# Expert gathers of a PEER layer on one core: down and up rows issued in alternating groups of four instead of eight

## The chip, the cores and the metric

One Trainium2 chip, one of its cores. The metric is the device time of one execution in microseconds (us); less is better.

## What is computed

One decoder layer for a prompt of 512 tokens and eight sample tokens: two parallel token mixers, then a PEER channel mixer, then a final norm. The change touches only PEER. For each token and each of eight heads a product-key search finds 16 experts out of 16,384. Each expert is one row of 1,024 fp32 numbers (4 KB) in `expert_down` and one in `expert_up`:

```python
    def block(xb):
        qv = (xb @ w_query).astype(f32).reshape(PEER_BLOCK, PEER_HEADS, 2, PEER_DHALF)
        s = jnp.einsum('thsd,hskd->thsk', qv, keys)
        sv, si = lax.top_k(s, PEER_TOPK)
        ...
        g = jax.nn.softmax(fv, axis=-1)
        u = expert_down[eidx]
        act = jax.nn.gelu(jnp.einsum('thkd,td->thk', u, xb).astype(f32), approximate=False) * g
        v = expert_up[eidx]
        return jnp.einsum('thk,thkd->td', act.astype(v.dtype), v)
```

## The kernel before

The program runs six stages, one after another. The last one, `stage_peer` (line 1527), begins some 975 us into the span and lasts to its end.

Its work is cut into 33 units. A unit is one head of one block of 128 tokens (4 blocks x 8 heads = 32), and between unit 19 and the one after it stands one unit for the samples, whose 8 tokens x 8 heads x 16 experts are 1,024 rows. A unit of the prompt has two steps of eight experts each, the samples' unit has one step, so there are NSTEP = 65 steps, numbered n = 0 to 64; the samples' step is n = 40. Step n needs eight down gathers D(n) and eight up gathers U(n). One gather is one indirect DMA issued by POOL: 128 rows of 4 KB, one into each partition, 512 KB. There are 520 of each kind.

What sets the order:

- **POOL** issues all gathers. In a loop over n it issues the eight of D(n) (`gather_down`, L1674), then the eight of U(n-4) (`gather_up`, L1694); LAG is 4. In the last step it issues D(64), then U(60) to U(64). Before the first gather of a unit it waits until the unit's expert numbers stand (`s_top`). Before every second down gather it waits until the buffer is free; down rows have a ring of 10 buffers in the first block and of 12 after it. Before the up gathers 0 and 4 of a step it waits until the same half of the eight up buffers has been used (`s_vused`).
- **DVE** multiplies each gathered down row with the token's row and sums (`products`, L1924, one instruction for one gather). For every unit it also picks the next unit's experts: `topk`, some 45 small instructions, of which L1916 writes the expert numbers. Its order in a unit is: products of the first step, stores of scores (L1371, first block only), `close` of a token block if one is due (L1944, L1946), topk of the next unit, products of the second step.
- **ACT** applies gelu and exp and spreads the weights into a diagonal form.
- **PE** multiplies the up rows with these weights and adds them up in PSUM (`add`, L1809; L1817 for the samples), four gathers to a half, with `s_vused` raised after each half. add(n-4) runs in step n. In the first block PE also projects and scores the queries of coming units (L1344, L1358): in an even step n up to 12 it scores two tiles through one PSUM bank before add(n-4), and the second score waits for DVE's store of the first. In step 14 it scores the samples and waits for DVE's copies after products(14) (L1987), then selects the samples' rows (L1826, L1828), then runs add(10).
- A token block is closed by DVE in steps 20, 36 and 53, after the products of that step: the multiply L1944 reads the PSUM banks that the next block's first add (add(16), add(32), add(49)) overwrites, and PE waits for it (`s_blkrd`).
- **SP** loads the query weights for the next units (1 MB each) and stores the closed blocks.

Of the kernel before, what the change touches and what calls it, by code (L numbers as in the profile page):

```python
# [55 lines left out]
PH = 8  # L56
# [1465 lines left out]
GATE = 8  # L1522
LAG = 4
VR = 8


def stage_peer(nc, mem, sem, ps, A, O, mod_d, integers):
# [54 lines left out]
    S = 2 * NU  # L1582
# [20 lines left out]
    at_step = {n: [n - LAG] for n in range(LAG, NSTEP)}  # L1603
# [3 lines left out]
    V_before = [max([m for m in range(n) if V_of[m] == V_of[n]], default=None) for n in range(NSTEP)]  # L1607
# [18 lines left out]
    with nc.Block() as block:  # L1626
        @block.sync
        def _(sp):
            for i in range(2, PH):
                if i > 2:  # L1630
                    sp.wait_ge(s_q, 2 * (i - 2))
                Q.load(sp, A, i).then_inc(s_w[i % 2], 16)
            sp.wait_ge(s_s, NQ)
            for dst, m in ((gate, 5), (shift, 6), (scale, 7)):
                sp.dma_start(dst[:, 0, :], mod_d[NS:NC_ROWS, m * D:(m + 1) * D].partition_broadcast(P)).then_inc(s_rows, 16)
                sp.dma_start(dst[0:NS, 1, :], mod_d[0:NS, m * D:(m + 1) * D]).then_inc(s_rows, 16)
            sp.dma_start(gf, A["g_final"].rearrange("(a n) -> a n", a=1).partition_broadcast(P)).then_inc(s_rows, 16)

            for i, b in enumerate(closings):
                sp.wait_ge(s_y, i + 1)  # L1640
                if b < NB:
                    sp.dma_start(O[0][0, b * P:(b + 1) * P, :], yb).then_inc(s_out, 16)
                else:
                    sp.dma_start(O[1].rearrange("b s d -> (b s) d"), yb[0:NS, :]).then_inc(s_out, 16)
            sp.wait_ge(s_out, 16 * (NB + 1))

        @block.gpsimd
        def _(pool):
            G = nc.gpsimd
            link = Link(pool, s_pc)  # L1650
            link(G.memset(Z, 0.0))
            link(G.memset(sel, 0.0))
            link(G.affine_select(out=sel, in_=sel, compare_op=ALU.not_equal, fill=1.0, base=0,
                                 pattern=[[0, 2 * PH], [-1, NS]], channel_multiplier=1))
            G.iota(iotai, pattern=[[1, TOPK]], base=0, channel_multiplier=0).then_inc(s_const, 1)  # L1655

            def gather_down(n):

                g = steps[n]
                u = unit_at[g]  # L1660
                if g == S or g % 2 == 0:
                    pool.wait_ge(s_top, u + 1)
                    pool.sem_inc(s_gatep, 1)
                if n == 2 * PH:
                    pool.wait_ge(s_ss, 1)
                    pool.sem_inc(s_gatep, 1)
                for j in range(GATE):
                    i = GATE * n + j
                    if j % 2 == 0 and U_free[i + 1] is not None:
                        pool.wait_ge(s_uused, U_free[i + 1] + 1)  # L1670
                        pool.sem_inc(s_gatep, 1)
                    k = (g % 2) * GATE + j
                    at = idxS[:, j:j + 1] if g == S else idx[u % 2][:, k:k + 1]
                    G.indirect_dma_start(U[i], None, down, bass.IndirectOffsetOnAxis(ap=at, axis=0))\  # L1674
                        .then_inc(s_U[U_sem[i][0]], 16)

            def gather_up(n):

                g, r = steps[n], V_of[n]
                if g != S and g % 4 == 0:  # L1680
                    pool.wait_ge(s_idxT, g // 4 + 1)
                    pool.sem_inc(s_gatep, 1)
                if r and V_before[n] is None:
                    pool.wait_ge(s_uused, GATE * NSTEP)
                    pool.sem_inc(s_gatep, 1)
                for j in range(VR):
                    if j % 4 == 0 and V_before[n] is not None:
                        pool.wait_ge(s_vused, 2 * V_before[n] + 1 + j // 4)
                        pool.sem_inc(s_gatep, 1)
                    if g == S:  # L1690
                        at = idxS[:, j:j + 1]
                    else:
                        at = idxT[(g // 4) % 2][:, VR * (g % 4) + j:VR * (g % 4) + j + 1]
                    G.indirect_dma_start(Vr[r][j], None, up, bass.IndirectOffsetOnAxis(ap=at, axis=0))\  # L1694
                        .then_inc(s_V[r][j], 16)

            for n in range(NSTEP):
                gather_down(n)
                for m in at_step.get(n, ()):
                    gather_up(m)  # L1700

        @block.scalar
        def _(act):
# [371 lines left out]
```

## Time and profile before

| | us |
|---|---|
| median of 3 runs | 2418.75 |
| lowest and highest | 2417.25, 2419.3 |
| the profiled execution | 2418.92 |
| its span, from its first to its last instruction | 2417.2 |
| PE, DVE, POOL busy in it | 1329.5, 1501.2, 1071.5 |
| DMA issued by POOL (queue q0) | 545.33 MB |

The span is cut by the page into 40 slices of 60.4 us; the mean busy share of the core's 16 DMA engines stands at 9 tenths or more in nearly every slice from the 19th on, which is where the gathers run. Matmul times are modelled by the profiler, and a DMA's landing is seen as the start of the instruction that waits for it.

### The profile page before, as it was taken

To read this page: it belongs to the slowest core of one execution; us is meant where nothing else is said; L and a number is where in the kernel's file an instruction comes from. 1 tells how busy PE (TensorE), PEld (TensorE's weight loads), DVE (VectorE), ACT (ScalarE), POOL (GpSimd) and SP (SyncE) were. 2 spreads that over 40 slices of the span, in tenths; PEclk is the share of its full clock that TensorE was granted. 3 is DMA by queue.
4 is the path that set the end of the run, shared out by engine and by line. 5 is a ranking of instruction groups with operands and counts; after the bars stand their busy time and mean duration, and the time that the engine had idled before them with its cause. 6 is when DMAs were issued, how large, how long until landed. Compare 5 with 4: busy or idle time off the path is not lost.

```text
span 2417.2 us, 19658 instructions
## 1 busy us (share of the span) xinstructions
PE 1329.5 (55%) x6380; PEld 763.6 (32%) x6380; DVE 1501.2 (62%) x3220; ACT 278.7 (12%) x567; POOL 1071.5 (44%) x1138
## 2 busy tenths in 40 slices
PE   3597997999754789656654333323332343232234
PEld 0276764778644654543431000000000010000000
DVE  0453999145488423686676777767686677676740
ACT  1111000111211002111110110000011011010100
POOL 0123000010031000357666777777775777777754
PEclk7898998899766999878885555566565565656657
DMA  9821100211133050589999999999998999999997
GB/s 365 320 64 67 39 35 0 90 40 72 53 96 129 12 193 1 183 334 405 406 403 409 409 402 409 410 409 405 406 406 319 409 384 409 409 410 409 409 369 287
DMA packets 208777, 651.97 MB, mean 270 GB/s; under 512 B 25936, under 2 KB 52208, under 8 KB 204537
## 3 DMA queue, kind: packets, MB, share of 16 engines
q0 software_dynamic: 149760, 545.33, 57.1%
q1 hardware_dynamic: 58092, 103.70, 12.0%
q10 hardware_dynamic: 824, 1.70, 0.2%
q8 instruction: 51, 0.84, 0.1%
q14 instruction: 50, 0.41, 0.0%
HBM read 643.24 MB, written 7.54 MB: 269 GB/s over the span
## 4 chain that ended last, share of the span: by engine, by line
DMA 20%; POOL 17%; issue 10%; DVE 8%; PE 4%; DVEq 1%; ACT 0%; POOLq 0%; ACTq 0%
DMA arena<-in_expert_up_dram,rows 13%; POOL arena L1694 9%; POOL arena L1674 8%; DMA arena<-in_expert_down_dram,expert 6%; DVE arena L1924 4%; PE ps L1809 3%; DMA arena<-in_expert_down_dram,sample 1%; DVE arena L1878 0%; DVE arena L1877 0%; DVEq L1871 0%; PE ps L1344 0%; PE ps L1358 0%; DVE keys L1876 0%; DVE arena L1905 0%; DVE arena L1902 0%
## 5 line engine op out<-in xcount | busy, mean ns | idle before, releaser
L1809 PE MATMUL ps<-arena 128*32 128x512 f32 x2048 | 413.4, 950 | 792.0 <-DMA arena<-in_expert_up_dram,rows 792.0
L1924 DVE CUSTOM_DVE_ANT_0 arena<-arena,ps 128x1024 f32<-128x1024 f32 x512 | 617.0, 1220 | 319.7 <-DMA arena<-in_expert_down_dram,expert 304.3
L1694 POOL DMA_INDIRECT arena<-in_expert_up_dram,rows x512 | 486.6, 950 | 217.0 <-issue 136.4
L1674 POOL DMA_INDIRECT arena<-in_expert_down_dram,expert x512 | 487.3, 952 | 207.2 <-issue 151.0
L1809 PEld LDWEIGHTS ps<-arena 128*32 128x32 f32 x2048 | 82.3, 147 | 1084.6 <-issue 1084.4
L546 PE MATMUL ps<-arena 128*128 128x260 f32 x896 | 204.9, 388 | 14.4 <-ACT arena L477 7.8
L546 PEld LDWEIGHTS ps<-arena 128*128 128x128 f32 x896 | 171.6, 193 | 51.1 <-issue 16.2
L954 POOL MEMSET arena<- 128x528 f32 x2 | 1.1, 537 | 305.5 <-POOLq L2044 305.5
L1344 PE MATMUL ps<-arena 128*128 128x260 f32 x512 | 123.9, 403 | 5.0 <-POOL counting L1655 3.6
L1071 PE MATMUL ps<-arena 128*128 128x260 f32 x512 | 112.5, 383 | 0.0
L1344 PEld LDWEIGHTS ps<-arena 128*128 128x128 f32 x512 | 101.8, 202 | 27.8 <-issue 5.1
L1071 PEld LDWEIGHTS ps<-arena 128*128 128x128 f32 x512 | 97.3, 190 | 14.8
L1714 ACT ACTIVATE arena<-arena 128x8 f32<-128x8 f32 x65 | 13.5, 208 | 729.4 <-DVE arena L1924 729.3
L970 POOL TENSOR_TENSOR arena<-arena 128x1024 f32<-128x1024 f32 x8 | 18.2, 2286 | 166.7 <-DVE arena L1230 127.1
L1460 PE MATMUL ps<-arena 128*128 128x512 f32 (+1 forms) x160 | 71.6, 611 | 7.9 <-DMA arena<-in_w_out_dram 7.9
L269 PE MATMUL ps<-arena 128*32 128x512 f32 x256 | 45.9, 855 | 47.2 <-DMA arena<-in_w_ada_dram 38.3
L1167 PE MATMUL ps<-arena 128*128 128x260 f32 x256 | 57.4, 388 | 0.0
L456 POOL MEMSET arena<- 128x4096 f32 x1 | 3.5, 3512 | 113.0 <-POOLq L2044 113.0
L469 POOL COPY arena<-arena 64x16 f32<-64x16 f32 x64 | 31.7, 547 | 48.2 <-DVE arena L720 48.1
L1167 PEld LDWEIGHTS ps<-arena 128*128 128x128 f32 x256 | 49.6, 194 | 7.8
L607 PE MATMUL ps<-arena 128*128 128x512 f32 x64 | 39.4, 751 | 21.1 <-DVE arena L737 12.6
L1419 POOL MEMSET arena<- 128x1024 f32 x1 | 1.0, 956 | 111.2 <-POOLq L2044 111.2
(352 smaller groups left out, 1858.1 us busy)
## 6 DMA issues: line engine op xcount, KB each, us to landing
arena<-in_w_ada_dram SPq DMA_DIRECT2D x12, 2048.0 KB, 19.7
arena<-in_w_in_dram SPq DMA_DIRECT2D x11, 2048.0 KB, 7.6
arena<-in_w_ada_final_dram SPq DMA_DIRECT2D x4, 2048.0 KB, 17.8
arena<-in_w_query_dram SPq DMA_DIRECT2D x8, 1024.0 KB, 16.9
arena<-in_expert_down_dram,expert POOLq DMA_INDIRECT x512, 12.3
arena<-in_expert_up_dram,rows POOLq DMA_INDIRECT x512, 12.0
out_dram<-arena SPq DMA_DIRECT2D x13, 512.0 KB, 3.0
arena<-in_x_prompt_dram SPq DMA_DIRECT2D x2, 2048.0 KB
```

What stands on the lines that cost most here:

```text
L269: last = nc.tensor.matmul(ps[strip(j, 32), i, :], cT[:, k, :], ring[q][:, k % 2, 512 * j:512 * j + 512], start=(k == 0), stop=(k == KD - 1))
L469: last = nc.gpsimd.tensor_copy(flat[:, 160 * q + 16 * g:160 * q + 16 * g + 16], bb[rows, j, 4 * ut + q, :])
L546: last = nc.tensor.matmul(ps[:, 5 + h, 0:HALF], ring[i % 2][:, k, m * P:(m + 1) * P], hT[:, k, h * HALF:(h + 1) * HALF], start=(k == 0), s ...
L607: last = nc.tensor.matmul(ps[:, 7, :], CT[j][:, i, :], S_of(i)[j].rearrange("p a b -> p (a b)"), start=(q == 0 and j == 0), stop=(q == 3 a ...
L1071: last = mm(ps[:, 2 * (n % 2) + h, 0:HALF], ring[i % 2][:, k, m * P:(m + 1) * P], hT[:, k, h * HALF:(h + 1) * HALF], start=(k == 0), stop= ...
L1167: last = mm(ps[:, 4 + 2 * (m % 2) + h, 0:HALF], brw[:, k, m * P:(m + 1) * P], cv[:, k, h * HALF:(h + 1) * HALF], start=(k == 0), stop=(k = ...
L1344: last = nc.tensor.matmul(ps[:, 2 + h, 0:HALF], self.ring[(t // 2) % 2][:, k, (t % 2) * P:(t % 2 + 1) * P], self.h2T[:, k, h * HALF:(h + 1 ...
L1460: last = mm(ps[0:n, 2 * (b % 2) + j, :], mg[:, k, b * P:b * P + n], wo[:, k, j * 512:(j + 1) * 512], start=(k == 0), stop=(k == KD - 1))
L1674: G.indirect_dma_start(U[i], None, down, bass.IndirectOffsetOnAxis(ap=at, axis=0))\
L1694: G.indirect_dma_start(Vr[r][j], None, up, bass.IndirectOffsetOnAxis(ap=at, axis=0))\
L1809: last = mm(ps[32 * j:32 * j + 32, c, :], Z[:, j, m, :], Vr[r][4 * half + j][:, c * 512:(c + 1) * 512], start=(p % 4 == 0 and m == 0), sto ...
L1924: V.tensor_tensor_reduce(U[i], U[i], row, 1.0, 0.0, ALU.mult, ALU.add, dots[n % 2][:, j:j + 1]).then_inc(s_uused, 1)
```

## The change

`gather_down` and `gather_up` take a part, 0 or 1, and issue four gathers instead of eight. In steps 4 to 63 POOL now issues D(n) 0-3, U(n-4) 0-3, D(n) 4-7, U(n-4) 4-7. In steps 0 to 3 there are no up gathers, and in step 64 D(64) is issued whole and then U(60) to U(64), each whole, so the order in those five steps is as before. The waits that stand ahead of a step's gathers go with part 0; the waits for buffers stay with their gathers. No buffer, semaphore, count or other engine's program is changed.

```diff
-            def gather_down(n):
+            def gather_down(n, part):
...
-                if g == S or g % 2 == 0:
+                if part == 0 and (g == S or g % 2 == 0):
                     pool.wait_ge(s_top, u + 1)
...
-                for j in range(GATE):
+                for j in range(4 * part, 4 * part + 4):
...
-            def gather_up(n):
+            def gather_up(n, part):
...
-                for j in range(VR):
+                for j in range(4 * part, 4 * part + 4):
                     if j % 4 == 0 and V_before[n] is not None:
                         pool.wait_ge(s_vused, 2 * V_before[n] + 1 + j // 4)
...
             for n in range(NSTEP):
-                gather_down(n)
-                for m in at_step.get(n, ()):
-                    gather_up(m)
+                up_now = at_step.get(n, ())
+                for part in range(2):
+                    gather_down(n, part)
+                    if len(up_now) == 1:
+                        gather_up(up_now[0], part)
+                if len(up_now) > 1:
+                    for m in up_now:
+                        for part in range(2):
+                            gather_up(m, part)
```

## Rows read from the trace of the kernel before

**Rows 1.** The page: the span, and what POOL's DMA queue carried (packets, MB, share).

```profile
span 2417.2 us, 19658 instructions
...
q0 software_dynamic: 149760, 545.33, 57.1%
```

**Rows 2.** Busy time by window: PE, PEld, DVE, ACT, POOL, PE clock, DMA share, GB/s.

```profile
1500.00:1510.00 10.00, 1.00 (x8) 0.40 (x12) 9.18 (x30) 1.49 (x2) 7.56 (x9) 0.52 1.03 409
...
1840.00:1850.00 10.00, 6.03 (x28) 1.37 (x32) 8.01 (x33) 1.29 (x7) 0.06 (x1) 0.50 0.16 66
1850.00:1860.00 10.00, 1.25 (x8) 0.00 (x0) 4.30 (x7) 2.29 (x7) 7.56 (x9) 0.50 0.81 278
...
1950.00:1960.00 10.00, 2.79 (x16) 0.54 (x16) 8.86 (x33) 4.37 (x9) 7.87 (x8) 0.72 0.82 277
```

**Rows 3.** POOL's waits for PE from 980 us: total us, times, longest us.

```profile
POOL arena L1694 <- PE ps L1809: 63.7, 50, 10.7
```

**Rows 4.** Timeline, an ordinary even step: start us, us, engine, line [idle before <- releaser].

```profile
1515.20 0.17 DVE L1916 CAST expert<-arena 128x16 uint32<-128x16 f32 x1
...
1522.30 0.94 POOL L1694 DMA_INDIRECT arena<-in_expert_up_dram,rows  x1 [0.30 <-issue]
1523.55 0.94 POOL L1674 DMA_INDIRECT arena<-in_expert_down_dram,expert  x1 [0.31 <-issue]
...
1535.75 1.22 DVE L1924 CUSTOM_DVE_ANT_0 arena<-arena,ps 128x1024 f32<-128x1024 f32 x1 [10.28 <-DMA arena<-in_expert_down_dram,expert]
```

**Rows 5.** Timeline, the samples' unit: last product, next experts, next down gather, its products.

```profile
1837.49 1.23 DVE L1924 CUSTOM_DVE_ANT_0 arena<-arena 128x1024 f32<-128x1024 f32 x1
...
1848.87 0.17 DVE L1916 CAST expert<-arena 128x16 uint32<-128x16 f32 x1
...
1849.94 0.93 POOL L1674 DMA_INDIRECT arena<-in_expert_down_dram,expert  x1 [12.91 <-DVE expert L1916]
...
1854.30 1.22 DVE L1924 CUSTOM_DVE_ANT_0 arena<-arena,ps 128x1024 f32<-128x1024 f32 x1 [5.02 <-DMA arena<-in_expert_down_dram,expert]
...
1864.66 1.22 DVE L1924 CUSTOM_DVE_ANT_0 arena<-arena,ps 128x1024 f32<-128x1024 f32 x1
```

**Rows 6.** Timeline, the samples' up rows on PE and POOL's next up gathers.

```profile
1933.31 15.45 PE L1817 MATMUL ps<-arena 128*8 128x512 f32 x31 [12.85 <-DMA arena<-in_expert_up_dram,sample]
...
1943.13 0.94 POOL L1694 DMA_INDIRECT arena<-in_expert_up_dram,rows  x1 [3.35 <-PE ps L1817]
...
1948.60 0.59 PE L1817 MATMUL ps<-arena 128*8 128x512 f32 x1
...
1950.00 0.94 POOL L1694 DMA_INDIRECT arena<-in_expert_up_dram,rows  x1 [2.20 <-PE ps L1817]
```

**Rows 7.** Timeline, step 14: last product, add(10), and add(11) one step later.

```profile
1294.35 1.22 DVE L1924 CUSTOM_DVE_ANT_0 arena<-arena,ps 128x1024 f32<-128x1024 f32 x1
...
1299.92 3.64 PE L1809 MATMUL ps<-arena 128*32 128x512 f32 x16
...
1320.98 3.64 PE L1809 MATMUL ps<-arena 128*32 128x512 f32 x16 [12.67 <-DMA arena<-in_expert_up_dram,rows]
```

**Rows 8.** Timeline, step 20: the closing multiply, add(16), and add(17) one step later.

```profile
1420.14 1.22 DVE L1944 TENSOR_TENSOR arena<-ps,arena 128x1024 f32<-128x1024 f32 x1
...
1424.24 3.64 PE L1809 MATMUL ps<-arena 128*32 128x512 f32 x16 [11.93 <-DMA arena<-in_expert_up_dram,rows]
...
1445.51 3.64 PE L1809 MATMUL ps<-arena 128*32 128x512 f32 x16 [12.89 <-DMA arena<-in_expert_up_dram,rows]
```

**Rows 9.** Timeline, step 10: last product, second score, add(6), and add(7).

```profile
1205.28 1.22 DVE L1924 CUSTOM_DVE_ANT_0 arena<-arena,ps 128x1024 f32<-128x1024 f32 x1
...
1207.33 2.05 PE L1358 MATMUL ps<-arena 128*128 128x128 f32 x8 [2.84 <-DVE arena L1371]
1210.51 3.49 PE L1809 MATMUL ps<-arena 128*32 128x512 f32 x16 [1.13 <-DMA arena<-in_expert_up_dram,rows]
...
1230.97 3.50 PE L1809 MATMUL ps<-arena 128*32 128x512 f32 x16 [6.21 <-DMA arena<-in_expert_up_dram,rows]
```

More of the change, by code:

```diff
@@ L1655, in _ @@
             G.iota(iotai, pattern=[[1, TOPK]], base=0, channel_multiplier=0).then_inc(s_const, 1)
-            def gather_down(n):
+            def gather_down(n, part):
                 g = steps[n]
                 u = unit_at[g]
-                if g == S or g % 2 == 0:
+                if part == 0 and (g == S or g % 2 == 0):
                     pool.wait_ge(s_top, u + 1)
                     pool.sem_inc(s_gatep, 1)
-                if n == 2 * PH:
+                if part == 0 and n == 2 * PH:
                     pool.wait_ge(s_ss, 1)
                     pool.sem_inc(s_gatep, 1)
-                for j in range(GATE):
+                for j in range(4 * part, 4 * part + 4):
                     i = GATE * n + j
@@ L1675, in gather_down @@
                         .then_inc(s_U[U_sem[i][0]], 16)
-            def gather_up(n):
+            def gather_up(n, part):
                 g, r = steps[n], V_of[n]
-                if g != S and g % 4 == 0:
+                if part == 0 and g != S and g % 4 == 0:
                     pool.wait_ge(s_idxT, g // 4 + 1)
                     pool.sem_inc(s_gatep, 1)
-                if r and V_before[n] is None:
+                if part == 0 and r and V_before[n] is None:
                     pool.wait_ge(s_uused, GATE * NSTEP)
                     pool.sem_inc(s_gatep, 1)
-                for j in range(VR):
+                for j in range(4 * part, 4 * part + 4):
                     if j % 4 == 0 and V_before[n] is not None:
```

## The prediction

> **What bounds the kernel now.** I read the page first, then busy time by window, then POOL's waits, then the timeline at the places where those two views disagree with an even flow. The page gives POOL's queue 545.33 MB [rows 1]; nothing in the change alters that. In an ordinary window the 16 DMA engines stand at a share of 1.03 and move 409 GB/s [rows 2]. At that rate one gather of 524,288 bytes takes 1.28 us. POOL starts one every 1.25 us [rows 4], a little faster, so it runs ahead until it meets a buffer that isn't free. Its waits for PE, 63.7 us in 50 of them [rows 3], are mostly this: a symptom of full DMA engines, not a cause of lost time. So the stage is bound by bytes through the DMA engines, and a wait of POOL costs time only if the engines run out of issued gathers.
>
> They do so in a few places. Around the samples, in 1840 to 1860, they moved 66 and 278 GB/s where 409 was possible: (818 - 344) / 409 x 10 = 11.6 us lost [rows 2]. In 1950 to 1960 they moved 277: (409 - 277) / 409 x 10 = 3.2 us lost [rows 2]. Another loss lies in the last step and one at the start of the stage, in whose steps the order isn't changed. I therefore look for the change's effect in two forms only: gathers that are late at a place where the engines already run dry, and places that newly run dry.
>
> **What the change moves.** It removes and adds no instruction. Gathers go through the engines in the order of issue, so I count in places of 1.28 us. Within a step the down gathers 4-7 are now four places later (+5.1 us) and the up gathers 0-3 four places earlier (-5.1 us); the others stay. From this follow two kinds of effect: what waits for the last down row of a step comes 5.1 us later, and POOL asks for the first half of the up buffers 5.1 us earlier. The distance from one use of an up buffer to the next stays 16 places, and from one use of a down buffer to the next it becomes more even, so where a buffer's user starts at landing nothing changes.
>
> **Ordinary steps: nothing.** The next unit's experts are written at 1515.20, and POOL wants them at 1523.55, 8.2 us later [rows 4]. The chain that writes them starts with the last down row, so the slack falls to about 3 us in ordinary units. Where it is less (steps with a close, or PE's scores in between) POOL may wait 1 to 3 us. But a gather's product starts 1535.75 - 1523.55 = 12.2 us after its issue [rows 4]: some eight issued gathers stand in line ahead of it, and the engines don't notice such a wait. I cost it at 0; without that cover each such wait would cost its 1 to 3 us.
>
> **The samples' unit: +5.1 us.** This unit has one step only, so topk of the next unit follows its products at once and POOL waits 12.91 us for it [rows 5], with the engines dry. The chain is: last down row of the samples, product 1.23, topk to L1916 at 1848.87, gather at 1849.94 [rows 5]. The last down row lands four places later, 4 x 1.28 = 5.1 us. The bytes issued before the wait are the same sixteen gathers in either order, so the engines run dry at the same moment and start again 5.1 us later. Nothing covers this. The one bound that could move it is the pace, 1.25 to 1.28 us a place: 5.0 to 5.1.
>
> **The samples' up rows: -3.2 us.** add(40) takes 15.45 us for 31 of its 32 matmuls [rows 6], much more than any other add, and it holds both halves of the up buffers: POOL waits 3.35 us, then 2.20 us [rows 6], and the engines lose 3.2 us [rows 2]. With the halves 5.1 us further apart, the first lands at 1933.3 - 5.1 = 1928.2, and PE has it done by 1937.2 (it took 1943.13 - 0.8 - 1933.31 = 9.0 us). POOL wants it at 1943.13 - 3.1 - 5.1 = 1934.9, so it waits some 3 us. The second half lands where it did, at 1933.3 + 5.1 = 1938.4, and is done 7 to 9 us later, by 1947; POOL wants it four up and four down gathers after the first, at about 1948. So of the two waits, which together emptied the line of issued gathers, one is left. I take the whole 3.2 us as won; bounds 0 and 3.2.
>
> **Places that newly run dry.** Here a thing that waits for the last down row holds PE, and with it the first half of the up buffers, which POOL now wants earlier. Before, from the last down row of step n to the first gather of U(n-3) there were 17 places, 21.8 us; now there are 9, 11.5 us. I work it out in landing times. The row by which add(n-4) started in the kernel before is the landing of its fourth up gather; that place now belongs to the last down gather of step n. The landing place of the first gather of U(n-3) is the start of the next step's add, less 3 places for its own fourth gather, less 4 for the move: less 9.0 us. From a release on PE to POOL's gather it takes 0.8 us (1949.19 to 1950.00 [rows 6]).
> - Step 14. From last product to add(10): 1299.92 - 1294.35 = 5.6 us, then the half of 3.64 and 0.8: 10.0 us [rows 7]. It starts at 1294.35 + 5.1 = 1299.5, so POOL issues U(11) at 1309.5. Its landing place is 1320.98 - 9.0 = 1312.0. Left: 2.5 us.
> - Step 20, closing. Product 1.22, multiply 1.22 [rows 8], add 3.64, 0.8: 7.0 us with the handovers. 1424.24 + 7.0 = 1431.2 against 1445.51 - 9.0 = 1436.5. Left: 5.3 us. The closings in steps 36 and 53 show the same pattern and leave 5.4 and 5.5.
> - Step 10. From last product to the end of the second score 1207.33 + 2.05 - 1205.28 = 4.1, then 3.49 and 0.8: 8.4 us [rows 9]. 1210.51 + 8.4 = 1218.9 against 1230.97 - 9.0 = 1222.0. Left: 3.1 us. In steps 6, 8 and 12, the same form of row, other DMAs (query weights, rows of the modulation) lie between and leave over 6 us.
>
> What must be left for the engines not to run dry? No row shows it for this pattern. From one side, the first gather after the dry spell reached its product 1854.30 - 1849.94 = 4.4 us after its issue [rows 5]. From the other, its eighth product began at 1864.66, 10.36 us after the first, where seven places are 8.96: so 1.4 us more went until the flow was full, 5.8 in all. I take 6.0, since it is the full flow that must be kept up, and keep 4.4 and 7.1 (5.8 and one more gather) as bounds. Lost then: step 14 3.5, step 10 2.9, closings 0.7 + 0.6 + 0.5 = 1.8; sum 8.2 us. With 4.4 it is 1.9 + 1.3 = 3.2 us; with 7.1 it is 4.6 + 4.0 + 5.1 = 13.7 us.
>
> At this point a rule of the Trainium skill bears: "DMA: Bandwidth & Descriptors", section on the anatomy of one DMA on the SWDGE path, gives a DMA issued from GpSimd a fixed 2.0 us plus its bytes at 436 GB/s, which is an estimated 3.2 us for one gather. This trace doesn't agree with it for the first gather after the dry spell, which took 4.4 us. By 3.2 the new dry places would cost an estimated 0.8 us in all; that is the first rival below.
>
> **Sum.** +5.1 - 3.2 + 8.2 = +10.1 us. The profiled execution took 2418.92 us, 1.7 more than its span, and the median is 2418.75, so nothing is to be corrected between them: 2418.75 + 10.1 = 2428.9 us.
>
> **Rivals.**
> - Short cover costs nothing: the engines need no more than 4.4 us of issued work or less, and PE's clock or an earlier product takes the rest at steps 10 and 14. For it speaks the 4.4 itself [rows 5]; against it the slow filling of the flow after it. It would leave +5.1 - 3.2 = +1.9 us, 2420.7: not slower by what can be measured. It decides from the point at which U(11) and U(7), issued 2.5 and 3.1 us ahead of their places, still land in them.
> - The stage is bound by POOL's issue, and each wait of POOL counts in full. POOL would wait some 9 us in steps 10 and 14 each and 5 to 7 at each of three closings, 36 us, and 5 at the samples: about 2460. Against it stands the share of 1.03 [rows 2] beside waits of POOL that add up to 63.7 us [rows 3].
> - The change wins: the 3.2 us at the samples' up rows are won, and at the samples' unit the last down rows come no later, because POOL has issued them so far ahead. Then 2415.5. But being ahead doesn't change the order of the transfers.
> - PE's clock: the adds run at the lower of its two levels in most windows (0.52, 0.50 [rows 2]; 3.64 us a half). If four even bursts changed what is granted, the holds at steps 10 and 14 would shrink or grow by 1 to 2 us each. This lies inside the range.
>
> **How the numbers follow.** The forecast's case, new dry places and a later samples' unit: 0.72, around 2428.9, from 2423.9 (+5.1 - 3.2 + 3.2) to 2434.4 (+5.1 - 3.2 + 13.7). Short cover free: 0.18. Issue-bound: 0.04. The change wins: 0.06. A difference of 0.2%, 4.8 us, is about what a measurement of this kernel can tell from no change. The first case lies above 2423.6 but for a small part (0.04 of it). So slower 0.73 with the issue-bound case, same 0.21, faster 0.06. For 8 in 10 the range reaches down into the second case and up to the first case's end: 2420 to 2434.
>
> **What would show it.** In the profile of the changed kernel: the wait of POOL's gather after the samples' products is 18 us instead of 12.91, and the two windows around it move about 5 us x 409 GB/s less. The waits behind L1817 are together 3 us or less, and no window there falls to 277. Up gathers of steps 14, 20, 36 and 53 have waits of 5 to 9 us on PE L1809, and windows right after them show less than 409. If windows there stay at 409, the second case holds. If ordinary windows show less than 405, the order itself costs bandwidth, and the sum is wrong as a whole.

## The result and the profile after

| | before | after |
|---|---|---|
| median, runs | 2417.84 us, 5 | 2433.09 us, 5 |
| lowest and highest | 2417.07, 2419.3 | 2428.24, 2435.69 |
| the profiled execution, its span | 2418.92, 2417.2 | 2433.09, 2431.3 |
| POOL's waits for PE in L1694 | 63.7 us in 50 | 73.2 us in 17 |

The ratio is 1.0061, with an interval of 1.0046 to 1.0075: slower by 15.25 us between the medians. The forecast was +10.1 us with a range up to 2434. Lines behind the edit stand six higher: L1815 is add, L1823 the samples' add, L1930 products, L1922 the writing of the expert numbers.

The page of the changed kernel: span and instructions, the DMA row and its GB/s in 40 slices, and POOL's queue.

```profile
span 2431.3 us, 19658 instructions
...
DMA  9811000211233050689999999999998999999997
GB/s 365 330 54 64 35 35 0 89 40 72 70 90 126 2 192 1 221 328 400 406 382 370 410 392 410 409 409 409 409 378 319 410 409 409 409 382 409 409 382 285
...
q0 software_dynamic: 149760, 545.33, 56.8%
```

Bytes and instruction count are those of [rows 1]. Most slices still hold 409. The slices below it are few and lie at known places: 382, 370 and 392 (the 21st, 22nd and 24th: steps 11 to 13, 14 and 20), 378 and 319 (steps 36 and 40), 382 (step 53); the last two hold the last step.

Busy time by window of the changed kernel: PE, PEld, DVE, ACT, POOL, PE clock, DMA share, GB/s. First an ordinary window, then the ones behind steps 14, 20, 36 and 53, then the samples' unit, then the samples' up rows.

```profile
1500.00:1510.00 10.00, 3.75 (x24) 1.16 (x24) 4.92 (x8) 0.87 (x4) 7.56 (x9) 0.50 1.03 409
...
1310.00:1320.00 10.00, 4.71 (x28) 0.91 (x20) 9.04 (x25) 1.68 (x3) 5.36 (x6) 0.67 0.58 199
1440.00:1450.00 10.00, 1.50 (x14) 0.26 (x9) 9.17 (x28) 3.17 (x5) 7.79 (x8) 0.67 0.93 306
1770.00:1780.00 10.00, 5.22 (x28) 1.08 (x20) 8.66 (x36) 4.11 (x6) 5.14 (x6) 0.67 0.69 247
2140.00:2150.00 10.00, 1.80 (x20) 0.31 (x12) 8.73 (x34) 2.98 (x6) 6.94 (x8) 0.82 0.73 252
...
1850.00:1860.00 10.00, 3.28 (x20) 0.68 (x16) 9.11 (x31) 1.49 (x2) 0.00 (x0) 0.50 0.52 207
1860.00:1870.00 10.00, 1.47 (x8) 0.00 (x0) 4.51 (x16) 3.32 (x11) 3.87 (x5) 0.50 0.32 100
...
1950.00:1960.00 10.00, 7.29 (x24) 1.55 (x23) 4.92 (x8) 0.00 (x0) 6.56 (x7) 1.00 1.03 408
```

The ordinary window shows the same 409 GB/s as [rows 2], so the order itself costs no bandwidth here. The four windows behind PE's holds fell, as the second kind of effect says. The 277 of before at the samples' up rows [rows 2] is gone.

Timeline of POOL in the changed kernel, the long waits ahead of up gathers behind steps 14, 20, 36, 40 (a down gather) and 53, then the samples' up rows: start us, us, engine, line [idle before <- releaser].

```profile
1313.12 1.22 POOL L1694 DMA_INDIRECT arena<-in_expert_up_dram,rows  x1 [9.62 <-PE ps L1815]
...
1438.68 0.94 POOL L1694 DMA_INDIRECT arena<-in_expert_up_dram,rows  x1 [6.06 <-PE ps L1815]
...
1773.34 0.93 POOL L1694 DMA_INDIRECT arena<-in_expert_up_dram,rows  x1 [8.45 <-PE ps L1815]
...
1864.91 0.94 POOL L1674 DMA_INDIRECT arena<-in_expert_down_dram,expert  x1 [15.67 <-DVE expert L1922]
...
1951.42 0.94 POOL L1694 DMA_INDIRECT arena<-in_expert_up_dram,rows  x1 [1.46 <-PE ps L1823]
...
2140.93 0.94 POOL L1694 DMA_INDIRECT arena<-in_expert_up_dram,rows  x1 [7.79 <-PE ps L1815]
```

There are others: ahead of the up gathers of steps 5, 7, 9, 11 and 13 POOL waits 5.60, 5.58, 4.15, 4.34 and 4.83 us for PE. The one in step 11 is the hold of step 10, which the forecast counted; the other four it put at nothing. Of many small waits for PE a few long ones have become: 17 with 73.2 us where there were 50 with 63.7 [rows 3].

**How I price a place.** The second half of each add starts, nearly everywhere, when the step's last up row has landed, and the place of that row in the order is the same in both kernels. (Not so in the changed kernel in even steps up to 14, where PE itself is late; none of them is used below.) So I take the start of that half on PE, less the start of the first gather of the stage, and subtract the same difference of before: the delay of the flow at that point. An example: in step 42 the second half starts at 1911.33 after and at 1896.40 before, the first gather at 986.74 and 989.20.

PE and POOL in the changed kernel:

```profile
986.74 1.16 POOL L1674 DMA_INDIRECT arena<-in_expert_down_dram,expert  x1 [11.68 <-DVE expert L1922]
...
1911.33 3.39 PE L1815 MATMUL ps<-arena 128*32 128x512 f32 x16 [7.25 <-DMA arena<-in_expert_up_dram,rows]
```

The same two in the kernel before:

```profile
989.20 1.16 POOL L1674 DMA_INDIRECT arena<-in_expert_down_dram,expert  x1 [11.69 <-DVE expert L1916]
...
1896.40 3.58 PE L1809 MATMUL ps<-arena 128*32 128x512 f32 x16 [1.48 <-DMA arena<-in_expert_up_dram,rows]
```

(1911.33 - 986.74) - (1896.40 - 989.20) = 17.4 us. Worked out so for five profiled kernels (the last four are told below), the delay in us at steps:

| kernel | 9 | 13 | 16 | 24 | 38 | 42 | 48 | 63 |
|---|---|---|---|---|---|---|---|---|
| after | 3.7 | 6.1 | 10.2 | 11.3 | 12.1 | 17.4 | 15.5 | 15.2 |
| h1_holds40 | 1.7 | 1.8 | 1.6 | 1.8 | 1.9 | 1.8 | -0.3 | -0.5 |
| k1_samples | 1.2 | 0.6 | 0.4 | 0.5 | 0.7 | 5.7 | 3.8 | 3.6 |
| k2_early40 | -0.1 | 0.1 | 0.0 | -0.2 | -0.2 | -3.3 | -5.5 | -5.7 |
| k3_step1415 | 1.1 | 1.1 | 4.5 | 3.9 | 4.4 | 3.9 | 2.7 | 2.3 |

Each row comes from one execution, set against one execution of the kernel before. Up to step 9 two of the four experiments have the order of before throughout and two have it in the even steps; they differ among themselves by 1.8 us, which is about the uncertainty of an early entry.

A part of every entry is older than the change. In steps 0 to 3 all kernels issue in the same order, and still D(4) doesn't start at the same time. Its first gather, in the changed kernel and in the kernel before:

```profile
1055.90 0.94 POOL L1674 DMA_INDIRECT arena<-in_expert_down_dram,expert  x1 [14.34 <-DVE expert L1922]
```

```profile
1056.16 0.94 POOL L1674 DMA_INDIRECT arena<-in_expert_down_dram,expert  x1 [12.96 <-DVE expert L1916]
```

That is 69.16 us after the stage's first gather in the changed kernel and 66.96 in the kernel before, so 2.2 us of the 3.7 at step 9 were there before the orders differ. The four experiments have 68.55, 68.24, 66.33 and 67.96 there (h1, k1, k2, k3): 1.6, 1.3, -0.6 and 1.0 us against the kernel before. From D(4) to step 9 the changed kernel loses 1.5 us and the experiments -0.1 to 0.5.

### The profile page after: what moved, and what is told of

Its sections match the earlier page's. It is cut to its first block, busy times and chain, and to the rows that moved or that the text cites. A ratio compares the mean times of both kernels' runs of the same rounds, so it can differ in the third digit from the quotient of the medians.

```text
span 2431.3 us, 19658 instructions
## 1 busy us (share of the span) xinstructions
PE 1348.8 (55%) x6380; PEld 769.7 (32%) x6380; DVE 1497.0 (62%) x3220; ACT 279.0 (11%) x567; POOL 1067.5 (44%) x1138
## 4 chain that ended last, share of the span: by engine, by line
POOL 22%; DMA 14%; issue 12%; DVE 8%; PE 4%; DVEq 1%; POOLq 0%; ACT 0%; ACTq 0%
POOL arena L1694 11%; POOL arena L1674 10%; DMA arena<-in_expert_down_dram,expert 8%; DMA arena<-in_expert_up_dram,rows 5%; DVE arena L1930 3%; PE ps L1815 3%; PE ps L1358 1%; DVE arena L1884 0%; DVE arena L1883 0%; DVEq L1877 0%; DMA arena<-in_expert_down_dram,sample 0%; DVE arena L1371 0%; PE ps L1823 0%; DMA arena<-in_expert_up_dram,sample 0%; DVE keys L1882 0%
## 5 line engine op out<-in xcount | busy, mean ns | idle before, releaser
L1815 PE MATMUL ps<-arena 128*32 128x512 f32 x2048 | 426.7, 982 | 771.9 <-DMA arena<-in_expert_up_dram,rows 729.3
L1930 DVE CUSTOM_DVE_ANT_0 arena<-arena,ps 128x1024 f32<-128x1024 f32 x512 | 613.6, 1219 | 337.7 <-DMA arena<-in_expert_down_dram,expert 326.2
L1694 POOL DMA_INDIRECT arena<-in_expert_up_dram,rows x512 | 483.2, 944 | 231.5 <-issue 150.1
L1815 PEld LDWEIGHTS ps<-arena 128*32 128x32 f32 x2048 | 84.8, 153 | 1067.2 <-issue 1067.2
L546 PE MATMUL ps<-arena 128*128 128x260 f32 x896 | 207.9, 391 | 14.5 <-ACT arena L477 7.8
L1344 PE MATMUL ps<-arena 128*128 128x260 f32 x512 | 126.4, 409 | 5.0 <-POOL counting L1655 3.6
L1071 PE MATMUL ps<-arena 128*128 128x260 f32 x512 | 112.5, 383 | 0.0
L269 PE MATMUL ps<-arena 128*32 128x512 f32 x256 | 48.9, 904 | 43.3 <-DMA arena<-in_w_ada_dram 34.8
L1167 PE MATMUL ps<-arena 128*128 128x260 f32 x256 | 57.4, 388 | 0.0
L1358 PE MATMUL ps<-arena 128*128 128x128 f32 x128 | 23.9, 347 | 53.0 <-DVE arena L1371 52.9
```

What stands on the lines that cost most here:

```text
L269: last = nc.tensor.matmul(ps[strip(j, 32), i, :], cT[:, k, :], ring[q][:, k % 2, 512 * j:512 * j + 512], start=(k == 0), stop=(k == KD - 1))
L546: last = nc.tensor.matmul(ps[:, 5 + h, 0:HALF], ring[i % 2][:, k, m * P:(m + 1) * P], hT[:, k, h * HALF:(h + 1) * HALF], start=(k == 0), s ...
L1071: last = mm(ps[:, 2 * (n % 2) + h, 0:HALF], ring[i % 2][:, k, m * P:(m + 1) * P], hT[:, k, h * HALF:(h + 1) * HALF], start=(k == 0), stop= ...
L1167: last = mm(ps[:, 4 + 2 * (m % 2) + h, 0:HALF], brw[:, k, m * P:(m + 1) * P], cv[:, k, h * HALF:(h + 1) * HALF], start=(k == 0), stop=(k = ...
L1344: last = nc.tensor.matmul(ps[:, 2 + h, 0:HALF], self.ring[(t // 2) % 2][:, k, (t % 2) * P:(t % 2 + 1) * P], self.h2T[:, k, h * HALF:(h + 1 ...
L1358: last = nc.tensor.matmul(ps[:, bank, b * P:(b + 1) * P], self.qT[t % 2][:, b * P:(b + 1) * P], self.kT[:, t, :], start=True, stop=True)
```

## The experiments

All kernels but g2 have the changed kernel's code with a set that names the steps in which the gathers alternate; in the others the order is that of before:

```diff
+            split = ...
             for n in range(NSTEP):
...
-                    if len(up_now) == 1:
+                    if n in split and len(up_now) == 1:
                         gather_up(up_now[0], part)
-                if len(up_now) > 1:
+                if n not in split or len(up_now) > 1:
```

In the recorded expectations theory A is that of the prediction, in which only places where something waits for a step's last down row cost time; rival B is an even cost of 15.25 / 60 = 0.25 us for each alternating step.

"Holds" are the ten steps in which PE or DVE keeps the first up half, or a unit is short: 4, 6, 8, 10, 12, 14, 20, 36, 53, and the samples' 40.

**Two kinds of flow.** The first eight experiments (e and g) ran on two chips on which the gathers flow less evenly, and the kernel before takes some 2585 us there. Busy time by window of e4_only4445, 100 us in which it has the order of before:

```profile
1500.00:1600.00 100.00, 30.87 (x156) 6.88 (x160) 57.07 (x145) 7.62 (x16) 66.69 (x70) 0.62 0.94 357
```

And of h1_holds40 on a chip with an even flow, with the order of after in the same stretch:

```profile
1500.00:1600.00 100.00, 34.12 (x168) 7.54 (x172) 68.23 (x177) 9.45 (x20) 74.42 (x79) 0.55 1.03 409
```

357 GB/s against 409. It isn't the order: g1_holds40, which alternates in this stretch, has 365 on such a chip, and the kernel before has 409 on the other kind. On those chips 1.5 to 1.7% of the gathers' packets took over 400 ns, on the others 0.3%, and runs of one kernel spread over some 30 us. What sets them apart, the chips themselves or something that went on beside the runs, no run shows. Each ratio is taken against the kernel before on the same chip. I tell the even-flow runs first, since the result comes from such a chip.

### h1_holds40: the ten holds in the order of before

```diff
+            split = set(range(4, 64)) - {4, 6, 8, 10, 12, 14, 20, 36, 40, 53}
```

> The changed kernel with D and U whole in steps 4, 6, 8, 10, 12, 14, 20, 36, 40 and 53 once more. On the chip of the experiments so far the gathers run at 350 to 370 GB/s, with 1.7% of the packets over 400 ns, against 409 GB/s and 0.3% in the profiles of the two kernels. If this run comes from an even flow (409 GB/s), theory A expects the kernel 2 to 3 us under the one before, and rival B (every alternating step costs 0.25 us) 12.5 us over it. If it comes from the uneven flow again, a theory D (the alternation takes cover from every step, and an uneven flow uses it up anywhere) expects the 13 us over the kernel before again.

Measured: 2418.87 us against 2418.95, ratio 0.9994 (0.9984 to 1.0005). Fifty of the 60 alternating steps are left, and the whole loss is gone. So on a chip with an even flow alternation costs nothing in ordinary steps (by landings the delay stays between 1.6 and 1.9 us from step 9 to 42 in the table), and what the change costs lies in the ten steps. The gain at the samples' up rows that theory A adds (-2 to -3) shows in the landings, 1.8 at step 42 to -0.3 at step 48. In the time it can't be told: the interval reaches from 3.9 us faster to 1.2 slower.

### k1_samples: alternation in the samples' step as well

```diff
+            split = set(range(4, 64)) - {4, 6, 8, 10, 12, 14, 20, 36, 53}
```

> The changed kernel with D and U whole in steps 4, 6, 8, 10, 12, 14, 20, 36 and 53; step 40 alternates. Beside the kernel in which step 40 is whole too (2418.87 us, 0.9994 of the kernel before) it differs in the samples' unit alone. Theory A: 5.1 us more than that one, 3 to 5 us over the kernel before, 2422 to 2424, and the whole shift comes between the landings of steps 39 and 41. Rival (the samples' unit is paid for by the idle engines): no more than 1 us over.

Measured: 2422.29 us against 2420.06, ratio 1.0012 (1.0002 to 1.0023). It differs from h1_holds40 by step 40 alone. The down gather behind the samples' products, on POOL, in k1_samples:

```profile
1859.72 0.94 POOL L1674 DMA_INDIRECT arena<-in_expert_down_dram,expert  x1 [16.90 <-DVE expert L1923]
```

and in h1_holds40:

```profile
1852.19 0.94 POOL L1674 DMA_INDIRECT arena<-in_expert_down_dram,expert  x1 [11.71 <-DVE expert L1923]
```

The wait is 5.2 us longer. From step 38 to 42 the landings slip 5.0 us in k1_samples and 0.1 the other way in h1_holds40. The ratios differ by 0.0018, 4.4 us, though each was taken on a chip of its own and has an interval of 0.001 to either side. This term is shown, at the size that was forecast.

### k3_step1415: alternation in steps 14 and 15 only

```diff
+            split = {14, 15}
```

> The kernel before with alternation in steps 14 and 15 alone: the last down row of step 14 four places later, and U(11) asked for four places earlier. Theory A: the scores of the samples, add(10) and U(11) follow the last down row and the DMA engines run dry for 3.5 to 4.1 us, as counted in landings: 2422 to 2423 us, with a wait of 9 to 10 us for PE ahead of U(11). A part of it may be given back later, where the kernel before has a lag among its DMA engines that this gap removes: then 2419 to 2421.

Measured: 2422.95 us against 2420.06, ratio 1.0019 (1.0009 to 1.0030): +2.9 us between the medians, +4.6 by the ratio. The timeline of PE and POOL:

```profile
1306.32 5.01 PE L1816 MATMUL ps<-arena 128*32 128x512 f32 x32
...
1310.47 0.94 POOL L1694 DMA_INDIRECT arena<-in_expert_up_dram,rows  x1 [5.76 <-PE ps L1816]
```

and the window around it:

```profile
1310.00:1320.00 10.00, 1.33 (x16) 0.12 (x4) 7.11 (x16) 0.74 (x1) 7.40 (x8) 0.80 0.74 246
```

The first gather of the stage starts at 989.68 here, so U(11) is issued 320.8 us after it; the forecast put it at 1309.5 - 989.2 = 320.3. The wait is 5.76 us and not the 9 to 10 that I expected, since POOL came to it later: it had waited 10.3 us for PE ahead of U(10). The landings slip from 1.1 at step 13 to 4.5 at step 16, 3.4 us; the forecast said 3.5. Of it 1.8 are given back by step 48 and 2.2 by step 63.

### k2_early40: the samples' down gathers eight places earlier

If the dry spell at the samples comes from the chain behind the samples' last down row, that row earlier must shorten it. Here D(40) is issued ahead of U(35) instead of behind it, and steps 44 and 45, which take over the samples' up buffers, alternate.

```diff
+            split = {44, 45}
             for n in range(NSTEP):
                 up_now = at_step.get(n, ())
+                if n == 40:
+                    gather_up(36, 0)
+                    gather_up(36, 1)
+                    continue
...
+                if n == 39:
+                    gather_down(40, 0)
+                    gather_down(40, 1)
```

> The kernel before with alternation in steps 44 and 45 alone, and D(40) issued ahead of U(35), eight places earlier, to see in an even flow what a dry spell is worth. If the slowest DMA engine sets the time, only the time between the last landing ahead of POOL's wait and the first after it is won, about 5.5 us, and with the 2 us of the samples' up rows the kernel takes 2410 to 2412 us. If what counts is the bytes that all engines together could have moved, 11.6 us are won there and the kernel takes 2404 to 2406. If the wait was hidden anyway: 2416.

Measured: 2414.4 us against 2420.06, ratio 0.9978 (0.9963 to 0.9992): faster than both kernels, by 0.2%. That is 5.3 us (1.9 to 9.0), where the expectation had 6 to 8 if the slowest engine sets the time and 12 to 14 if bytes do. POOL and PE in k2_early40 around the samples' step, and the windows 1830 to 1850:

```profile
1808.43 0.94 POOL L1674 DMA_INDIRECT arena<-in_expert_down_dram,sample  x1 [3.95 <-DVEq L1885]
...
1832.09 3.27 PE L1823 MATMUL ps<-arena 128*32 128x512 f32 x16 [24.23 <-DMA arena<-in_expert_up_dram,rows]
1836.20 0.94 POOL L1694 DMA_INDIRECT arena<-in_expert_up_dram,rows  x1 [5.93 <-PE ps L1823]
...
1846.14 0.94 POOL L1674 DMA_INDIRECT arena<-in_expert_down_dram,expert  x1 [0.30 <-issue]
```

```profile
1830.00:1840.00 10.00, 5.31 (x40) 1.49 (x40) 6.88 (x26) 0.75 (x4) 3.15 (x5) 0.76 0.65 242
1840.00:1850.00 10.00, 3.64 (x16) 0.68 (x16) 0.76 (x5) 4.93 (x14) 7.56 (x9) 0.58 0.98 354
```

The wait for the expert numbers is gone: the down gather at 1846.14 waits for issue alone. But U(35) now lies eight places later, so add(35) starts later, its buffers come free later, and U(36) waits 5.93 us for PE with the flow running dry at 242 GB/s. POOL also waits 3.95 us ahead of D(40) itself. The stall was moved and cut, not removed: 3.1 us are won by step 42, 2.2 more by step 48 at the samples' up rows. Since a new gap took the place of the old one, this run doesn't decide between the two forms of the expectation.

### The eight runs on the chips with an uneven flow

| kernel | median | before | ratio | interval |
|---|---|---|---|---|
| e1_whole40 | 2606.03 | 2587.44 | 1.0068 | 1.0045 to 1.0091 |
| e2_holds | 2601.22 | 2587.44 | 1.0069 | 1.0044 to 1.0095 |
| g4_holds | 2600.52 | 2584.36 | 1.0065 | 1.0035 to 1.0094 |
| g1_holds40 | 2597.51 | 2584.36 | 1.0050 | 1.0014 to 1.0085 |
| e3_ordinary | 2590.89 | 2587.44 | 1.0019 | 0.9989 to 1.0048 |
| e4_only4445 | 2585.6 | 2587.44 | 0.9992 | 0.9966 to 1.0019 |
| g2_pairs | 2633.45 | 2584.36 | 1.0185 | 1.0119 to 1.0251 |
| g3_early40 | 2589.84 | 2584.36 | 1.0006 | 0.9970 to 1.0043 |

**e1_whole40** leaves out step 40 alone, `split = set(range(4, 64)) - {40}`.

> The changed kernel with one step undone: in step 40, the samples' unit, D(40) is issued whole and then U(36) whole; all other steps alternate. Theory A (the time comes from things that wait for the last down row of a step, moved four places of 1.28 us): the samples' part, +5.1 us, goes, so 2433.1 - 5.1 = 2428 us, and POOL's wait after the samples' products is about 5 us shorter. Rival B (alternating as such costs bandwidth or issue, evenly over the 60 steps, 15.25 / 60 = 0.25 us a step): 2432.8 us. Rival C (everything lies in the places that newly run dry, and the samples' unit costs nothing): 2433 us.

+17.6 us by the ratio (11.6 to 23.5), where theory A had 10 and both rivals 15: it misses theory A.

**e2_holds** is the kernel of k1_samples; g4_holds is the same again, on the other chip.

> The changed kernel with D(n) and U(n-4) whole in steps 4, 6, 8, 10, 12, 14 (PE's scores wait for the last down row), 20, 36 and 53 (closings); the other 51 steps alternate, the samples' unit too. Theory A: only the samples' unit (+5.1) and the samples' up rows (-2 to -3.2) are left, so 2417.8 + 5.1 - 2.6 = 2420.3 us, between 2419.5 and 2422, and the waits of 4 to 10 us for PE in steps 5 to 15, 21, 37 and 54 are gone. Rival B (evenly 0.25 us a step): 51 x 0.25 = 12.8, 2430.6 us. Rival C: 2418 us or less.

> The changed kernel with D and U whole in steps 4, 6, 8, 10, 12, 14, 20, 36 and 53 alone (step 40 alternates), to be read beside the kernel in which step 40 is whole too. Theory A: the difference between the two is the samples' unit alone, 5.1 us; this one is 2 to 3 us over the kernel before. Rival B: the two are 0.25 us apart, 12.8 over the kernel before.

+17.9 and +16.8 us by the ratios, where theory A had 2 to 4 and rival B 12.8: a clear miss for theory A here. The samples' unit alone does show: from step 38 to 42 the delay grows by 12.3 and 13.9 us in these two, which alternate in step 40, and by 6.0 to 9.2 in e1, e3, e4 and g1, which don't.

**g1_holds40** is the kernel of h1_holds40.

> The changed kernel with D and U whole in steps 4, 6, 8, 10, 12, 14, 20, 36, 53 and in step 40 too; the other 50 steps alternate. Theory A (only what waits for the last down row of a step costs): all costs are gone and the samples' up rows' 2 to 3 us are won: 2 to 3 us under the kernel before. Rival B (alternation costs evenly, 0.25 us a step): 12.5 us over it.

With every hold in the order of before, 13 us stay (+0.50%), where the same program shows nothing at an even flow. So here alternation costs something that isn't in the ten steps, and theory A fails on these chips.

**e3_ordinary** alternates in fifteen ordinary steps, `split = set(range(21, 36))`.

> The kernel before with alternation in steps 21 to 35 alone, where no close, score or samples' work lies. Theory A: nothing waits there with less cover than 6 us, so no change: 2417.8 us within 1 us. Rival B (0.25 us a step): 2421.6 us. A theory in which even spacing of down and up rows helps the buffers would give less than 2416.

+3.5 us, but the interval includes no difference, and both theories (0 and +3.8 us) lie in it. It isn't against a cost of some 0.26 us per alternating step, which is what g1_holds40 would give if its loss were spread evenly over its fifty steps (13 / 50); it doesn't show one either.

**e4_only4445** alternates in the two steps behind the samples only, `split = {44, 45}`.

> The kernel before with alternation in steps 44 and 45 alone, where the samples' up rows and the ones that follow them are gathered. Theory A: the second wait behind the samples' add goes and 2.0 to 3.2 us are won: 2414.6 to 2415.8 us; faster than both kernels. Rival B: 0.5 us slower, 2418.3 us.

-1.8 us, the sign that was expected, within the uncertainty.

**g2_pairs** issues in groups of two instead of four, in all steps:

```diff
-                for j in range(4 * part, 4 * part + 4):
+                for j in range(2 * part, 2 * part + 2):
...
-                for part in range(2):
+                for part in range(4):
```

> The changed kernel with groups of two instead of four, in the same steps: the last down row of a step comes two places (2.6 us) later still, and the first up row is asked for two places earlier. Theory A: in the samples' unit 2.6 us more; at every hold of PE that already costs time (steps 11, 15, 21, 37, 54) 5.1 us more, 25.6 in all; at steps 5, 7, 9 and 13, where cover was just used up, 3 to 5 us each, 14 to 17 in all; so 42 to 48 us over the changed kernel and 57 to 63 over the kernel before. Rival B (a cost per step or per switch between down and up, of which there are now twice as many): 30 us over the kernel before. If the ordinary steps suffer too, more than 65.

Measured +48 us (1.0185 of 2584.36). The direction is sure, more mixing costs more. The size falls between the two numbers that were expected, and it was taken where the flow is uneven, so it tells the theories apart only weakly.

**g3_early40** is the kernel of k2_early40.

> The kernel before with alternation in steps 44 and 45 alone, and with the samples' down gathers D(40) issued ahead of U(35), eight places earlier. Theory A in its two forms: POOL's wait after the samples' products shrinks from 12.9 to some 3 us. If the slowest of the 16 DMA engines sets the time (a gather lands when its slowest part has), only the time in which no gather is left to land is won there, about 5.5 us, and with the samples' up rows' 2 the kernel is 7.5 us faster than before. If the bytes count that all engines together could have moved in 1840 to 1860, 11.6 us are won there and 14 in all. Rival C (that wait is hidden): 2 to 3 us faster only.

No difference that these runs can tell.

**Where the loss lies.** It isn't spread evenly. By landings, worked out as above and against the same profile of the kernel before (with an even flow, so that all numbers are large), the delay grows from step 9 to 17 by 24.1 to 31.1 us in e2, g1 and g4, which alternate in the odd steps there, and by 17.0 to 17.5 in e3, e4 and g3, which don't alternate there at all. From step 17 to 38 it grows by 48.6 to 50.4 in the first three and by 54.8 and 55.3 in e4 and g3. So the extra stands in the first block, where PE is busy with scores, and nothing points at the ordinary steps behind it. A set that leaves the even step whole and alternates in the odd one behind it still asks for the first up half four places earlier, right behind PE's hold. In g1_holds40, ahead of U(9) in step 13:

```profile
1305.37 1.19 POOL L1694 DMA_INDIRECT arena<-in_expert_up_dram,rows  x1 [9.85 <-PE ps L1816]
```

In e2 and g4 this wait is 9.76 and 8.99 us, in e3 and e4 4.03 and 4.07. That these waits are what costs the time is an argument from one execution of each kernel: no experiment undoes the odd steps alone, and the cause stays open.

## Why the prediction came out as it did

The sign and the two mechanisms were right, and so were all named places but the closing in step 53, which cost about nothing instead of 0.5 us. The time lies in the range by 0.9 us, and two of the five runs (2435.41, 2435.69) lie above it, so that the number came out inside is in part luck. The sum was 4.6 us too small against the ratio of the runs (0.0061 x 2417.84 = 14.7 us against 10.1). By landings, in us:

| step of the prediction | forecast | measured in after | where shown alone |
|---|---|---|---|
| steps 0 to 3, same order | 0 | +2.2 (the experiments -0.6 to +1.6) | not a place of the change |
| steps 4 to 9 | 0 | +1.5 (the experiments -0.1 to +0.5) | no |
| step 10 to 13 | +2.9 | +2.4 | no |
| step 14 | +3.5 | +4.1 | k3_step1415, +3.4 |
| closings 20, 36, 53 | +1.8 | +1.1, +0.8 (1.3 from step 35 to 38), about 0 | no |
| samples' unit | +5.1 | +5.3 | k1 against h1, +5.0 to +5.1 |
| samples' up rows | -3.2 | -1.9 | k2_early40, -2.2 |

**Bound by bytes, not by issue: right.** POOL waits 9.5 us longer for PE in all and the time grows by 15; the place that costs most, the samples' unit, isn't among these waits. The issue-bound rival is out (2460).

**Ordinary steps at nothing: right at an even flow** (h1_holds40). Where the flow is uneven something outside the ten steps costs 13 us (g1_holds40), by landings in the first block.

**The samples' unit: right in size, wrong in its wait.** I said a wait of 18 us and it is 15.67. The gather is late by the forecast amount, but POOL also reaches the wait later, since POOL runs less far ahead in the changed kernel. The wait of an issuer isn't a measure of the loss; the landings are.

**The samples' up rows: over-sized.** Of the two waits one is left, 1.46 us, and no window falls to 277: the mechanism held. The forecast took the 3.2 us that a window's bytes showed as won. The landings gain 1.9. This is the term of the sum that was most over-sized. And the loss of before isn't a fixed one: in k3_step1415, which has the old order there, the window of the same stretch reads 359 instead of 277 GB/s, (409 - 359) / 409 x 10 = 1.2 us, and the one behind it 390, 0.5 us more, with PE's granted clock at 0.88 in the first where [rows 2] has 0.72. So by bytes there are 1.7 to 3.2 us to be won there. How much may hang on how fast add(40) runs; that it is the clock was not tried.

```profile
1950.00:1960.00 10.00, 5.13 (x28) 1.42 (x29) 9.25 (x27) 3.50 (x8) 6.06 (x7) 0.88 0.96 359
```

**Steps 4 to 9 at nothing: too little.** "In steps 6, 8 and 12 ... leave over 6 us" put these three at 0, and step 4, which has the same hold, isn't named at all. The changed kernel waits behind all four as it does behind step 10. POOL ahead of U(1), U(3), U(5) and U(9), behind steps 4, 6, 8 and 12:

```profile
1086.04 0.94 POOL L1694 DMA_INDIRECT arena<-in_expert_up_dram,rows  x1 [5.60 <-PE ps L1815]
...
1131.05 0.94 POOL L1694 DMA_INDIRECT arena<-in_expert_up_dram,rows  x1 [5.58 <-PE ps L1815]
...
1174.98 0.94 POOL L1694 DMA_INDIRECT arena<-in_expert_up_dram,rows  x1 [4.15 <-PE ps L1815]
...
1263.83 0.94 POOL L1694 DMA_INDIRECT arena<-in_expert_up_dram,rows  x1 [4.83 <-PE ps L1815]
```

But a wait isn't a loss. The windows right behind the first three:

```profile
1090.00:1100.00 10.00, 6.04 (x35) 3.73 (x33) 9.51 (x20) 2.09 (x3) 7.56 (x9) 1.00 0.98 365
1130.00:1140.00 10.00, 9.33 (x52) 6.49 (x48) 8.67 (x32) 0.98 (x3) 6.90 (x7) 1.00 1.01 382
1180.00:1190.00 10.00, 4.98 (x30) 2.79 (x29) 9.70 (x20) 2.10 (x3) 7.86 (x8) 1.00 1.03 410
```

The kernel before has 409, 405 and 409 in them. Behind step 4 that is 1.1 us by bytes, behind step 6 0.7 and 0.3 more in the next window (395), and the landings agree about so: 1.5 us from D(4) to step 9. Step 8 costs nothing, and neither does step 12: the delay is 6.1 us at step 13 as at step 11. So the forecast was right for steps 8 and 12, and short by some 1.5 us in all for steps 4 and 6. What they cost alone I didn't run.

**Where the rest of the sum's error comes from.** Measured from D(4) on, the landings lose 13.0 us by step 63 and not 10.1. The 2.9 missing are 1.5 in steps 4 to 9 and 1.3 at the samples' up rows; the misses at steps 10 and 14, at the closings and in the samples' unit (-0.5, +0.6, -0.2, +0.2) all but cancel. The other 2.2 us of the landings came about in steps 0 to 3. The six executions on chips with an even flow spread over 2.8 us there, so I don't put it down to the change.

**Needed cover, 6.0 us: right.** Step 14 had 2.5 us left and lost 3.4 to 4.1, which makes 5.9 to 6.6; step 10 had 3.1 left and lost 2.4, which makes 5.5. The first rival (4.4 is enough) would have it lose 1.9 or less; it is out, since in k3_step1415 POOL issued at the time that was worked out and the flow lost 3.4 all the same. The estimate from the Trainium skill's "DMA: Bandwidth & Descriptors" (the SWDGE path in the anatomy of one DMA), 3.2 us, would make it about 0.7; this case's runs don't agree with it.

**PE's clock.** The five runs of after differ by 7.5 us where those of before differ by 2.2, and the slowest two have the lowest mean clock (0.725, against 0.741 in the fastest). PE's holds now stand ahead of long waits of POOL in nine places, so this fits; it is a correlation over five runs and not shown.

## What to carry to other kernels

Before a queue's order is changed, list for every resource the issuer will now want earlier: who holds it, until when, and how many places of issued work lie between (in this kernel the list left out step 4, whose hold has the form of the others); a place with less than about 6 us of issued work loses the difference, and a place where other traffic blurs that distance needs bounds of its own in the sum (here steps 4, 6, 8 and 12 cost 0 to 1 us each). A finer alternation doesn't smooth anything if each kind has a ring of its own: it moves the last row of one kind and the first of the other, and what matters is only who waits for these two. And price a stall by when the next data lands, not by the issuer's wait and not by the bytes missing from a window. Start the count at a point up to which both orders are still the same: what differs there isn't the change's.

## What the runs showed of the hardware

**The DMA engines drift apart.** The bytes missing from a window overstate the time lost. In after, behind step 36, the window shows 247 GB/s, (409 - 247) / 409 x 10 = 4.0 us, and the landings slip 1.3 (from 10.8 at step 35 to 12.1 at step 38); behind step 53 it is 252, 3.8 us, and about nothing; behind step 14 it is 199, 5.1 us, and 4.1. In before, the window 1840 to 1850 has a DMA share of 0.16, 66 GB/s [rows 2], as if next to nothing were under way, and still PE waits in it for a row of an up gather:

```profile
1842.62 3.64 PE L1809 MATMUL ps<-arena 128*32 128x512 f32 x16 [11.33 <-DMA arena<-in_expert_up_dram,rows]
1847.61 3.64 PE L1809 MATMUL ps<-arena 128*32 128x512 f32 x16 [1.35 <-DMA arena<-in_expert_up_dram,rows]
```

A share of 0.16 is 2.6 of 16 engines. Each gather counts its semaphore up in 16 parts, and it has landed when the last of them has. By the semaphore events of the trace of before, the first and the last part of one up gather (the sixth of U(n-4)) are 8.3 us apart in step 39, 1.3 in step 41, behind the dry spell, and 6.7 in step 63: some parts fall behind as long as the flow is full. Counted from the time by which as many bytes had moved, the last row of step 39 lands 7.9 us late and that of step 41 1.1. A short gap late in such a stretch is taken up by the engines that were ahead, and the slowest, which has work left, loses little. That is how I read why the closings in steps 36 and 53 cost less than their windows show: in after, the lag counted so falls from 5.0 us in step 36 to 1.6 in step 38. h1_holds40 shows it best. It has step 36 in the order of before and alternates in step 37, POOL waits 5.00 us there, and the window behind it:

```profile
1760.00:1770.00 10.00, 5.35 (x32) 1.17 (x32) 8.66 (x35) 3.44 (x6) 4.24 (x5) 0.83 0.73 273
```

By bytes that is (409 - 273) / 409 x 10 = 3.3 us, and the next window, 355, has 1.3 more. The landings don't slip at all (2.0 us at step 35, 1.9 at step 38), and the time of the kernel is that of before.

**The same program isn't equally fast everywhere.** It took about 2418 us in some sets of runs and about 2585 in others, each set on one chip, with gathers at 409 and at 350 to 370 GB/s, and a change that is free in the one (h1_holds40) costs 0.5% in the other (g1_holds40). Whether that is the chip isn't shown.
